# Unrolled expert loop, early output halves, four-bank scatter and ScalarE table loads in a two-layer encoder kernel

## The chip, the cores and the metric

One core of one Trainium2 chip runs the whole program. The metric is device time in microseconds (us) of one execution; lower is better. Engines are named as the profile names them: PE (TensorE matmuls), PEld (TensorE weight loads, which overlap PE), DVE (VectorE), ACT (ScalarE), POOL (GpSimd), SP (SyncE). A "q" behind a name (SPq, PEldq) is the engine's sequencer: its branches, register work and DMA issues.

## The reference

256 tokens of 1024 float32 features pass two layers. Only the last sub-layer and the input matter for the change:

```python
for i in range(DEPTH):                       # DEPTH = 2
    h = rms_norm(x, ln_mix[i])
    x = x + (dilated_attention(h, ...) if i == 0 else rwkv7_bidirectional(h, ...))
    h = rms_norm(x, ln_ffn[i])
    x = x + (swiglu(h, f_w13, f_w2) if i == 0 else moe_swiglu(h, m_router, m_w13, m_w2))

def moe_swiglu(h, router, w13, w2):
    logits = t @ router                      # 8 experts, the two best per token
    combine = softmax over the two, 0 elsewhere
    for e in range(8):
        out = out + combine[:, e:e+1] * swiglu(t, w13[e], w2[e])   # 1024 -> 2 x 3584 -> 1024
```

The kernel takes the rows of a token only to its two experts. Each expert has room for 96 rows (CAP); more go to an overflow loop of at most 5 turns (OVER), and for these inputs it has nothing to do.

## The kernel before

All weights are streamed once from HBM through a ring of R = 6 slots of 2 MB in SBUF. SP issues each unit as two DMAs of 1 MB (`halves`, line 475) after waiting until TensorE is done with the slot's last content (`wait_free`, `wait_free_e`, lines 449 to 462). The order of the work is written out by hand, one block of code for each engine, with semaphores between them.

**Start.** SP issues x in two halves (line 499), then five small tables (lines 500 to 504: the identity matrix and frequencies `const`, the gains `vec`, positions, two tables of QK gains), then the first weight units (line 505 on). VectorE waits for both halves of x and for `vec` (lines 1663 to 1665) ahead of its first instruction; TensorE waits for `const` (line 772), transposes the normalised x (line 695), then starts the QKV projection (line 800) once unit 0 is in its slot.

**Experts.** `expert_plan` gives each expert 21 units: 14 "up" (lines 1252 to 1262, matmuls of lines 1258 and 1261) and 7 "down" (lines 1271 and 1275). Experts 0 to 5 run in a hardware loop of three turns with two experts in each, on TensorE (line 1286), ScalarE (1576) and VectorE (2183). SP's loads run ahead, so the first pair is written out there and the loop of line 643 has two turns. Experts 6 and 7 are written out on every engine. Experts 0 to 6 store their result in DRAM (`yd`) from where GpSimd gathers each token's rows (line 2372); VectorE adds them to x in `add_rows` while TensorE works on expert 7.

**End.** Expert 7's result goes back to x by `scatter` (lines 1235 to 1243): four matmuls, two in each of the PSUM banks 4 and 7, with the third and fourth waiting until VectorE's `add_back` (line 2095) has read the bank. Then each engine reads the number of overflows (`value_load`) and goes five times through the overflow loop, skipping the body each time by a branch. After its loop VectorE raises `experts_done` (line 2199), and SP stores the whole of x in one DMA (line 667) and waits for it.

```python
            with pe.Fori(0, EXPERTS // 2 - 1) as i:          # 1286
                for e in range(2):
                    one_expert(i * 2 + e, e, i)
...
            dve.memset(over_f, 0.0).then_inc(experts_done, 1)   # 2199
...
            sp.wait_ge(experts_done, 1)                         # 666
            sp.dma_start(out.rearrange("(t p) n -> p t n", p=P), x).then_inc(out_done, 16)
            sp.wait_ge(out_done, 16)
```

## Time and profile before

| | us |
|---|---|
| runs, median of 3 (lowest, highest) | 1990.71 (1987.49, 1991.77) |
| the profiled execution | 1985.81 |
| its span in the trace | 1983.9 |
| granted TensorE clock over the span | 0.985 of full speed |
| PE busy | 1886.6 (95%) |
| DVE busy, ACT busy, POOL busy | 703.3, 279.6, 198.3 |
| HBM read | 460.04 MB, 237 GB/s over the span |

The span runs from the first to the last event of the trace; the 1.9 us between it and the execution's time lie around it. The trace gives each instruction's start and length, what released a waiting one, and the chain of releases that ended last. The expert stage runs from about 1025 us to 1969 us, so nearly half of the span.

### The profile page before, as it was taken

What the parts mean: (1) busy time and instruction counts of PE and PEld (TensorE: products, weight loads), DVE (VectorE), ACT (ScalarE), POOL (GpSimd) and SP (SyncE); (2) the same over time, 40 slices, a digit from 0 to 9 for tenths busy, and PEclk for the clock granted to TensorE, in tenths of its full rate; (3) what the DMA queues carried; (4) which work ended last, traced back from release to release, by engine and by line L of the source; (5) the groups of instructions that cost most, each with busy time, mean ns of one, the idle gap of its engine ahead of it and who ended that gap; (6) DMA issues with size and microseconds to landing.
All of it is one profiled execution on the core that took longest, in us unless ns stands there. A gap on an engine that the chain in (4) does not pass through costs nothing.

```text
span 1983.9 us, 42949 instructions
## 1 busy us (share of the span) xinstructions
PE 1886.6 (95%) x18932; PEld 1188.0 (60%) x18932; DVE 703.3 (35%) x2063; ACT 279.6 (14%) x557; POOL 198.3 (10%) x318
## 2 busy tenths in 40 slices
PE   7999998999998999998979999899998999999997
PEld 3445445677754568877665565555555555565554
DVE  3123213100017356675353434233342333424332
ACT  2112112100000324542200000000000000000000
POOL 1111110100001414653010000000000000000000
PEclk9999999999998999999979999999999999999999
DMA  9441441644532100103359999899998999999992
GB/s 360 160 148 65 158 138 43 192 168 146 167 127 85 38 16 16 33 15 94 130 208 405 407 389 398 333 393 379 398 387 331 391 389 394 380 395 397 400 371 89
DMA packets 137658, 472.98 MB, mean 238 GB/s; under 512 B 30104, under 2 KB 59056, under 8 KB 94464
## 3 DMA queue, kind: packets, MB, share of 16 engines
q1 hardware_dynamic: 134592, 460.05, 61.5%
q0 software_dynamic: 2080, 7.37, 1.1%
q8 instruction: 156, 2.56, 0.5%
q10 hardware_dynamic: 800, 2.76, 0.3%
q14 instruction: 30, 0.25, 0.0%
HBM read 460.04 MB, written 10.10 MB: 237 GB/s over the span
## 4 chain that ended last, share of the span: by engine, by line
PE 87%; DVE 6%; ACT 2%; DMA 2%; issue 2%; SPq 0%; POOL 0%; DVEq 0%; POOLq 0%
PE ps L1258 19%; PE ps L678 13%; PE ps L800 13%; PE ps L1261 10%; PE ps L1271 10%; PE ps L738 8%; PE ps L1275 5%; PE ps L751 3%; PE ps L854 1%; PE ps L767 1%; DMA arena<-yd,arena 1%; PE ps L1198 1%; DVE arena L1860 1%; PE ps L686 1%; PE ps L1205 1%
## 5 line engine op out<-in xcount | busy, mean ns | idle before, releaser
L1258 PE MATMUL ps<-arena 128*64 128x256 f32 x3584 | 415.2, 384 | 13.6 <-issue 12.9
L678 PE MATMUL ps<-arena 128*128 128x128 f32 (+11 forms) x2114 | 332.4, 331 | 33.4 <-DVE arena L1847 9.1
L1258 PEld LDWEIGHTS ps<-arena 128*64 128x64 f32 x3584 | 249.0, 138 | 161.3 <-issue 49.6
L678 PEld LDWEIGHTS ps<-arena 128*128 128x128 f32 (+4 forms) x2114 | 247.5, 186 | 110.1 <-issue 55.5
L800 PE MATMUL ps<-arena 128*128 128x512 f32 x576 | 253.1, 595 | 1.9 <-DMA arena<-wqkv 1.9
L2115 DVE TENSOR_TENSOR arena<-arena,ps 64x384 f32<-64x384 f32 x112 | 62.3, 558 | 518.5 <-ACT arena L1560 518.4
L1261 PE MATMUL ps<-arena 128*32 128x128 f32 x7168 | 219.0, 274 | 0.0
L1261 PEld LDWEIGHTS ps<-arena 128*32 128x32 f32 x7168 | 188.9, 110 | 43.1 <-issue 43.1
L1271 PE MATMUL ps<-arena 128*64 128x512 f32 x896 | 207.0, 604 | 4.2 <-DVE arena L2107 4.2
L800 PEld LDWEIGHTS ps<-arena 128*128 128x128 f32 x576 | 108.0, 191 | 128.4 <-issue 125.6
L1560 ACT ACTIVATE arena<-ps 64x384 f32<-64x384 f32 x112 | 54.1, 483 | 799.3 <-PE ps L1261 799.3
L738 PE MATMUL ps<-arena 128*128 128x256 f32 x704 | 153.7, 381 | 0.0
L738 PEld LDWEIGHTS ps<-arena 128*128 128x128 f32 x704 | 134.4, 191 | 20.1 <-issue 1.9
L2106 DVE STREAM_TRANSPOSE arena<-arena 32x128 f32<-32x128 f32 x448 | 136.3, 304 | 9.9
L1271 PEld LDWEIGHTS ps<-arena 128*64 128x64 f32 x896 | 60.1, 138 | 114.4 <-issue 114.4
L1275 PE MATMUL ps<-arena 128*32 128x256 f32 x1792 | 108.3, 382 | 0.0
L1275 PEld LDWEIGHTS ps<-arena 128*32 128x32 f32 x1792 | 52.6, 109 | 74.2 <-issue 45.4
L2107 DVE STREAM_TRANSPOSE arena<-arena 32x64 f32<-32x64 f32 x448 | 87.6, 196 | 0.0
L2372 POOL DMA_INDIRECT arena<-yd,arena x4 | 3.8, 956 | 825.1 <-DMA yd<-arena 824.2
L1656 DVE TENSOR_TENSOR arena<-arena,ps 128x256 f32<-128x256 f32 x22 | 9.3, 421 | 198.4 <-ACT arena L1329 198.4
L1702 DVE TENSOR_REDUCE arena<-arena 128x4 f32<-128x512 f32 x24 | 16.5, 686 | 130.4 <-ACT arena L1354 130.4
L751 PE MATMUL ps<-arena 128*128 128x512 f32 x128 | 55.6, 592 | 0.0
(249 smaller groups left out, 1225.9 us busy)
## 6 DMA issues: line engine op xcount, KB each, us to landing
arena<-mw SPq DMA_DIRECT2D x336, 1024.0 KB, 8.2
arena<-wqkv SPq DMA_DIRECT2D x36, 1024.0 KB, 7.5
arena<-fw SPq DMA_DIRECT2D x32, 1024.0 KB, 6.6
arena<-wrkv SPq DMA_DIRECT2D x12, 1024.0 KB, 7.4
arena<-awo SPq DMA_DIRECT2D x4, 1024.0 KB, 6.3
arena<-bwo SPq DMA_DIRECT2D x4, 1024.0 KB, 9.9
xg<-arena POOLq DMA_DIRECT2D x8, 384.0 KB, 9.0
arena<-xg SPq DMA_DIRECT2D x7, 384.0 KB, 11.5
```

The costliest lines, as they stand in the source:

```text
L678: last = mm(o, a, b, start=(n == 0), stop=(n == len(pairs) - 1))
L738: last = mm(ps[:, c % 4, side * S:(side + 1) * S], w[:, k, side * S + f * P:side * S + (f + 1) * P], src[:, k, :], start=(k == 0), stop=(k ...
L751: last = mm(ps[:, 4 + 2 * t + h, :], hid[:, n % 2, k, t * P:(t + 1) * P], w[:, k, h * 512:(h + 1) * 512], start=(n == 0 and k == 0), stop= ...
L800: last = mm(ps[:, 4 + c % 2, :], hT[:, k, t * P:(t + 1) * P], w[:, k, :], start=(k == 0), stop=(k == KB - 1))
L1258: mm(ps[r, g % 4, 0:256], picked[:, b, k, 0:64], w[:, k, a * 256:(a + 1) * 256], start=(k == 0), stop=(k == KB - 1))
L1261: last = mm(ps[r, g % 4, 256:384], picked[:, b, k, 64:CAP], w[:, k, a * P:(a + 1) * P], start=(k == 0), stop=(k == KB - 1))
L1271: mm(ps[r, 5, :], hidT[:, g % 2, k, 0:64], w[:, k, a * 512:(a + 1) * 512], start=(first and k == 0), stop=(end and k == 3), skip_group_che ...
L1275: last = mm(ps[r, 6, 0:256], hidT[:, g % 2, k, 64:CAP], w[:, k, a * 256:(a + 1) * 256], start=(first and k == 0), stop=(end and k == 3), s ...
L1560: act.activation(sg_e[RH:P, g % 2, :], ps[0:RH, g % 4, 0:3 * P], ACT.Silu).then_inc(sge_sb, 1)
L2106: dve.transpose(o[:, :, :, 32 * i:32 * i + 32], low[:, :, :, j, :])
L2107: last = dve.transpose(o[:, :, i, 64:CAP], high[:, :, j, :])
L2115: dve.tensor_tensor(hid_e[RH:P, pair % 2, g % 2, :], sg_e[RH:P, g % 2, :], ps[RH:P, g % 4, 0:3 * P], ALU.mult).then_inc(hide_sb, 1)
```

## The change

1. ScalarE issues the five small tables, `vec` first, as its first instructions; on SP the first weight unit follows x directly.
2. The loop over experts is gone on TensorE, ScalarE, VectorE and SP: the same three pairs are written out.
3. The scatter writes to banks 4, 7, 0 and 1, and TensorE waits for no addition in between.
4. SP stores x in two halves, each once its own two additions are done, ahead of its overflow loop. A turn of the overflow loop, if one is needed, stores both halves again. `experts_done` is gone.

```diff
@@ SP
             for t in range(T):
                 sp.dma_start(x[:, t, :], x_in[t * P:(t + 1) * P, :]).then_inc(in_x[t], 16)
-            sp.dma_start(const[:, 0:C_TRI], const_in[:, 0:C_TRI]).then_inc(in_const, 16)
-            sp.dma_start(vec, vec_in).then_inc(in_vec, 16)
-            sp.dma_start(pos_i, pos_in).then_inc(in_small, 16)
-            sp.dma_start(qkc, qk_cols).then_inc(in_small, 16)
-            sp.dma_start(qkr, qk_rows.partition_broadcast(P)).then_inc(in_small, 16)
             for u in range(U_QKV):
...
-            with sp.Fori(1, EXPERTS // 2 - 1) as i:
+            for i in range(1, EXPERTS // 2 - 1):
...
+            for t in range(T):
+                sp.wait_ge(back_sb, 2 * t + 2)
+                sp.dma_start(out[t * P:(t + 1) * P, :], x[:, t, :]).then_inc(out_done, 16)
             sp.wait_ge(over_ok, 1)
             many = sp.value_load(over_i[0:1, 0:1], min_val=0, max_val=OVER)
             with sp.Fori(0, OVER) as j:
                 with sp.If(j < many):
...
+                    sp.wait_ge(out_done, j * 32 + 32)
...
+                    for t in range(T):
+                        sp.wait_ge(back_sb, j * 4 + (2 * t + 6))
+                        sp.dma_start(out[t * P:(t + 1) * P, :], x[:, t, :]).then_inc(out_done, 16)
-            sp.wait_ge(experts_done, 1)
-            sp.dma_start(out.rearrange("(t p) n -> p t n", p=P), x).then_inc(out_done, 16)
-            sp.wait_ge(out_done, 16)
+            sp.wait_ge(out_done, 32)
@@ TensorE, scatter
-                    if k >= 2:
-                        pe.wait_ge(back_sb, back * 4 + (k - 5))
-                    run(ps[:, (4, 7)[k % 2], :], [(pickT[0:width, b, t, :], yb[0:width, h * 512:(h + 1) * 512])]).then_inc(back_ps, 1)
+                    run(ps[:, (4, 7, 0, 1)[k], :], [(pickT[0:width, b, t, :], yb[0:width, h * 512:(h + 1) * 512])]).then_inc(back_ps, 1)
@@ TensorE, experts (ScalarE and VectorE likewise)
-            with pe.Fori(0, EXPERTS // 2 - 1) as i:
+            for i in range(EXPERTS // 2 - 1):
                 for e in range(2):
                     one_expert(i * 2 + e, e, i)
@@ ScalarE
+            act.dma_start(vec, vec_in).then_inc(in_vec, 16)
+            act.dma_start(const[:, 0:C_TRI], const_in[:, 0:C_TRI]).then_inc(in_const, 16)
+            act.dma_start(pos_i, pos_in).then_inc(in_small, 16)
+            act.dma_start(qkc, qk_cols).then_inc(in_small, 16)
+            act.dma_start(qkr, qk_rows.partition_broadcast(P)).then_inc(in_small, 16)
@@ VectorE
-                    dve.scalar_tensor_tensor(x[:, t, cols], ps[:, (4, 7)[n % 2], :], weight(t), x[:, t, cols], ALU.mult, ALU.add).then_inc(back_sb, 1)
+                    dve.scalar_tensor_tensor(x[:, t, cols], ps[:, (4, 7, 0, 1)[n], :], weight(t), x[:, t, cols], ALU.mult, ALU.add).then_inc(back_sb, 1)
...
-            dve.memset(over_f, 0.0).then_inc(experts_done, 1)
+                    dve.wait_ge(out_done, j * 32 + 64)
+                    dve.memset(over_f, 0.0)
```

What the compiled programs show. The start of SP's program before, and then of SP's and ScalarE's in the changed kernel (line numbers are each kernel's own; 475 and 474 are the helper that issues weights):

```order
L499 DMA arena<-x 128x1024 x2
L500 DMA arena<-const 128x144
L501 DMA arena<-vec 128x96
L502 DMA arena<-pos 128x2
L503 DMA arena<-qk_cols 128x6
L504 DMA arena<-qk_rows 128x192
L475 DMA arena<-wqkv 128x4x512 x12
L507 DMA arena<-const 128x1730
```

```order
L498 DMA arena<-x 128x1024 x2
L474 DMA arena<-wqkv 128x4x512 x12
L501 DMA arena<-const 128x1730
```

```order
L1309 DMA arena<-vec 128x96
L1310 DMA arena<-const 128x144
L1311 DMA arena<-pos 128x2
L1312 DMA arena<-qk_cols 128x6
L1313 DMA arena<-qk_rows 128x192
L1324 ACT_TABLE_LOAD
L1324 ACTIVATE arena<-arena 128x1024 x2
```

Five issues have gone from between x and the first weights on SP, and stand ahead of ScalarE's first table load.

TensorE at the end of expert 1 (and, in the loop, of 3 and 5), before and then changed. `REGISTER_ALU` and the branch are the loop's; before, the row behind the branch is reached only after the third turn:

```order
L1271 MATMUL ps<-arena 64x512 x8
L1275 MATMUL ps<-arena 32x256 x16
L1286 REGISTER_ALU
L1286 COMPARE_AND_BRANCH
L1258 MATMUL ps<-arena 64x256 x16
```

```order
L1268 MATMUL ps<-arena 64x512 x8
L1272 MATMUL ps<-arena 32x256 x16
L1255 MATMUL ps<-arena 64x256 x16
L1258 MATMUL ps<-arena 32x128 x32
L1255 MATMUL ps<-arena 64x256 x16
```

The next expert's first matmuls now stand directly behind the last of the one before.

TensorE's scatter (the MATMUL rows) before and then changed, followed by SP's end, before and then changed (`[waits ...]` are the semaphores an instruction waits for):

```order
L678 MATMUL ps<-arena 128x512 [waits pickT_sb,result_sb]
L678 MATMUL ps<-arena 128x512
L678 MATMUL ps<-arena 128x512 [waits back_sb] x2
L1294 TENSOR_LOAD arena [waits over_ok]
```

```order
L677 MATMUL ps<-arena 128x512 [waits pickT_sb,result_sb]
L677 MATMUL ps<-arena 128x512 x3
L1291 TENSOR_LOAD arena [waits over_ok]
```

```order
L655 REGISTER_ALU
L655 COMPARE_AND_BRANCH
L667 DMA out<-arena 128x2x1024 [waits experts_done]
```

```order
L649 DMA out<-arena 128x1024 [waits back_sb] x2
L651 TENSOR_LOAD arena [waits over_ok]
```

The store has moved from behind the overflow loop to ahead of it, and is in two pieces.

## Rows read from the trace of the kernel before

**Rows 1.** Page, part 1: busy us of each engine, share of the span, instructions
```profile
PE 1886.6 (95%) x18932; PEld 1188.0 (60%) x18932; DVE 703.3 (35%) x2063; ACT 279.6 (14%) x557; POOL 198.3 (10%) x318
```

**Rows 2.** Chain of waits, expert 1's first matmuls: start us, us, what
```profile
1140.16 3.60 PE ps L1258 x32
```

**Rows 3.** The chain at the first jump back, expert 1 to 2
```profile
1255.15 4.01 issue
1259.16 4.50 PE ps L1258 x24
1263.65 1.82 issue
...
1266.56 1.89 PE ps L1261 x64
```

**Rows 4.** The chain at the second jump back (3 to 4), and leaving the loop
```profile
1492.93 5.50 issue
...
1505.43 1.89 PE ps L1261 x64
...
1731.80 3.60 PE ps L1258 x32
```

**Rows 5.** The loops' branches, on TensorE and VectorE: count, min/median/max ns, starts
```profile
L1286 PEldq COMPARE_BRANCH  x3: 83/5078/6573, 1253.8 to 1730.4; - x3
...
L2183 DVEq COMPARE_BRANCH  x3: 50/56/67, 1255.3 to 1732.0; - x3
```

**Rows 6.** Stretches: us, busy PE, PEld, DVE, ACT, POOL; clock, DMA share, GB/s
```profile
1264.70:1280.70 16.00, 15.22 (x276) 1.00 0.70 263
...
1025.10:1255.10 230.00, 230.00 (x3360) 137.17 (x3360) 93.42 (x372) 14.71 (x30) 4.02 (x4) 1.00 0.98 387
```

**Rows 7.** DMA: issues 1025 to 1060, 1180 to 1255 (us to landing); total 1020 to 1975
```profile
arena<-mw SPq DMA_DIRECT2D x12, 1024.0 KB, 11.0
...
arena<-mw SPq DMA_DIRECT2D x26, 1024.0 KB, 7.9
...
DMA packets 49500, 351.39 MB, mean 368 GB/s; under 512 B 5536, under 2 KB 5536, under 8 KB 7904
```

**Rows 8.** The chain at the start
```profile
1.65 0.42 SPq L500
...
4.01 0.43 SPq L475
...
4.49 9.31 DMA arena<-wqkv
```

**Rows 9.** Timeline at the start: ScalarE's first squares, TensorE's transposes
```profile
4.44 1.06 ACT L1321 ACTIVATE arena<-arena 128x1024 f32<-128x1024 f32 x1 [2.43 <-DMA arena<-x]
...
8.34 3.65 PE L695 MATMUL ps<-arena 128*128 128x128 f32 x16 [8.34 <-DVE arena L1625]
```

**Rows 10.** The stretch in which the small tables arrive (columns of rows 6)
```profile
5.00:8.00 3.00, 0.00 (x0) 0.00 (x0) 0.72 (x2) 2.79 (x5) 0.57 (x1) 1.00 0.91 200
```

**Rows 11.** Timeline of VectorE at the end
```profile
1973.76 1.61 DVE L2095 SCALAR_TENSOR_TENSOR arena<-ps,arena 128x512 f32<-128x512 f32 x2 [0.36 <-PE ps L678]
1979.35 0.07 DVE L2199 MEMSET arena<- 128x11 f32 x1 [3.98 <-issue]
```

**Rows 12.** The end by line: TensorE's and SP's sequencers (ns), the store's landing
```profile
L1294 PEldq TENSOR_LOAD <-arena x1: 487/487/487, 1973.5 to 1973.5; - x1
...
L1297 PEldq COMPARE_BRANCH  x5: 221/221/3520, 1974.5 to 1980.9; - x5
...
L149 PEldq DRAIN  x1: 8/8/8, 1981.5 to 1981.5; - x1
...
L654 SPq TENSOR_LOAD <-arena x1: 480/480/480, 1936.5 to 1936.5; - x1
...
L655 SPq COMPARE_BRANCH  x5: 40/45/54, 1938.1 to 1940.7; - x5
...
DMA to landing us min/median/max: 4.0/4.0/4.0
```

More of the change, by code:

```diff
@@ L364, in build @@
             sem(n) for n in ("up_ps", "sge_sb", "hide_sb", "rows_turned", "hidT_sb", "down_ps", "result_sb", "back_ps", "back_sb"))
-        experts_done = sem("experts_done")
         in_lora, d_ready, mix_ready, mix_ps, mix_sb, ones_ok = (sem(n) for n in ("in_lora", "d_ready", "mix_ready", "mix_ps", "mix_sb", "ones_ok"))
@@ L1575, in _ @@
             act.dma_start(yd[(EXPERTS - 1) * CAP:, :].rearrange("o (a n) -> (o a) n", n=P), zero[0:KB, :]).then_inc(yd_out, 16)
-            with act.Fori(0, EXPERTS // 2 - 1) as i:
+            for i in range(EXPERTS // 2 - 1):
                 for e in range(2):
@@ L2182, in _ @@
             overflow_list()
-            with dve.Fori(0, EXPERTS // 2 - 1) as i:
+            for i in range(EXPERTS // 2 - 1):
                 for e in range(2):
```

## The prediction

> **What bounds the kernel now.** I read the page first: TensorE is busy 1886.6 of 1983.9 us, the next engine 703.3 [rows 1]. So only what makes TensorE pause, and what lies before its first and after its last matmul, can be worth anything here. Then the chain of waits, followed through the expert stage. Within experts it is TensorE's own work without a gap: the first group of an "up" unit takes 3.60 us [rows 2], and the whole first turn of the loop, two experts, takes 230.05 us, from 1025.10 to 1255.15, with TensorE busy throughout [rows 3, 6]. The chain breaks at the loop's jumps back. After expert 1 TensorE has nothing to do for 4.01 us, starts, does 24 matmuls of its first group in 4.50 us, pauses another 1.82 us, and only at 1266.56 reaches the second group [rows 3]. The second jump reads alike: 5.50 us, then the second group at 1505.43 [rows 4]. Where the loop is left, the next group starts at 1731.80 and takes the plain 3.60 us [rows 4].
>
> The rows of the branches say what this is. TensorE's sequencer needs 6573 and 5078 ns for the two branches that go back and 83 ns for the one that falls through; VectorE's need 50 to 67 ns [rows 5]. No semaphore stands behind these waits ("issue"), and the data are there. The Trainium skill, "Runtime: NRT & Kernel Launch", section "Instruction fetch mechanics", has a rule for it: code is fetched ahead in sequence, and a taken branch to a page that isn't held must wait for a fetch. By that rule straight code has none of the pauses, and the skip over the overflow body, also a taken branch, keeps its own. Without it one could as well read the pauses as the price of starting a pair of experts, and the loop's term would be nothing (rival 3). Long for the jumps back and short for the fall-through is what the rule asks for, so the trace agrees.
>
> **The change, part by part.** The durations are those of the profiled execution, 1985.81 us, which is 4.90 us under the median of the runs; the sum is taken from both.
>
> *No loop over experts.* From the end of expert 1 to the second group: 1266.56 - 1255.15 = 11.41 us where 3.60 would do, so 7.81 us lost. At the second jump 1505.43 - 1492.93 = 12.50, so 8.90 us lost. What follows is unharmed: from 1505.43 to 1731.80 are 226.4 us, and the first turn without its first group is 230.05 - 3.60 = 226.4. In the changed program the rows at this place are those of the crossing from expert 0 to 1 or of the fall-through, and neither shows any pause. Gain **16.7 us**. Bounds: 25% more if the pauses of other executions are longer, and 5.5 less if one fetch pause of the longer kind remains: 11 to 21. The loops of the other engines cost TensorE nothing: their branches take at most 67 ns and lie beside 230 us of matmuls.
>
> The cover that could go is the weight stream, since the pauses let it catch up: in the 16 us after the first jump the DMA engines are busy only 0.70 of the time, against 0.98 and 387 GB/s over a turn [rows 6]. I look at the landings. Right after the first pair starts a DMA lands 11.0 us after its issue, 150 us later, with no pause in between, 7.9 us after [rows 7]. A backlog would lengthen these. A slot is issued when the unit six places ahead is done, so it has about five units of 230.05 / 42 = 5.48 us, 27 us. So 27 - 8 = 19 us are in hand, and stay. Cost nothing.
>
> *Tables on ScalarE.* TensorE's transposes end at 8.34 + 3.65 = 11.99 us [rows 9] and its first projection waits to about 13.80 for unit 0, issued from 4.01 us on [rows 8]. In the change unit 0 is issued where L500 stood, at 1.65: 2.36 us earlier, the upper bound. But what moves is the issue, not the transfers: while the tables arrive the DMA engines are already busy 0.91 of the time, at 200 GB/s only [rows 10], because small pieces take engine time too. If none of it overlaps with weights, the gain is the idle part, 0.09 x 3 us = 0.3. If the missing bytes, (387 - 200) / 387 of 3 us, are all filled, it is 1.4. I take **0.9**, between them. The lower end is a loss: identity and `vec` now share the engines with 2 MB of weights, and if the identity took the 9.31 us of [rows 8] from an issue at about 1.2, transposes would run from 10.5 to 14.2, about 0.4 late. On ScalarE the five issues, (4.01 - 1.65) / 5 = 0.47 each, stand ahead of its activation table load and of the squares, which now start at 4.44, when x is in [rows 9]. Should they come 1 us later, the transposes end by 13.0, still about when unit 0 lands; so that costs nothing. Range -0.4 to 2.4. Here the Trainium skill speaks for less than the issue rows promise: "DMA: Bandwidth & Descriptors", section "Issuing engines are not separate DMA queues", says that issuing from several engines saves only the sequencer's time, as all use the same 16 DMA engines. Taken alone it would give the whole 2.4 and a sum 1.5 larger; no run here shows the two queues side by side at the start.
>
> *Four banks.* VectorE's four additions stand in two pairs, the second of 1.61 us, with 0.36 between [rows 11]. Without the wait the last ends some 0.3 earlier, at 1975.07 instead of 1975.37. This counts in the next part.
>
> *The end.* Now: additions end 1975.37, VectorE's five skipped turns to 1979.35, then the store, 4.0 us to landing [rows 11, 12], span 1983.9. Changed: SP issues the second half at about 1975.1, it lands by 1979.1 even at the 4.0 us of the whole, and SP then has its own loop still to go. That took from 1936.5 to 1940.8, 4.3 us, hidden under matmuls [rows 12]; now it starts behind the issue at 1975.6 and ends at 1979.9. VectorE ends at 1979.05. TensorE has the heaviest skip, 3.52 us for its first branch, and drained at 1981.5, having begun to read the count at 1973.5 [rows 12], just behind its waits on the additions. Without these it begins 0.4 to 2.2 us earlier (a matmul's issue, or the start of the scatter), so it ends between 1979.3 and 1981.1. So what was behind the store is late next: SP's loop or TensorE's. Latest of the three about 1980.2, and the closing exchange of signals took 0.4 (the store landed at 1979.45 + 4.0 = 1983.45). New end 1980.6, gain **3.3 us**, from 2.4 to 4.0.
>
> Sum: 16.7 + 0.9 + 3.3 = **20.9 us**. From the profiled execution 1985.81 - 20.9 = 1964.9; from the median 1990.71 - 20.9 = **1969.8 us**. The bounds give 13.0 to 27.4, so 1963.3 to 1977.7.
>
> **The rivals.**
> 1. *Only the loop pays.* Tables and weights get in each other's way at the start, and TensorE's overflow loop, whose skip is a fetch too, ends no earlier than 1983.5. For it: 0.91 busy in [rows 10], 3.52 us in [rows 12]. 16.7 alone: 1974.0.
> 2. *Dearer pauses.* The two pauses differ by 1.1 us, a fetch has to queue behind weight DMAs, and the median lies 4.9 us above the profiled run. If that difference was in the jumps, it goes too: 25.8, 1964.9.
> 3. *The pauses move or stay.* The long straight code could pay for its fetches somewhere else, if the trouble were fetching under full DMA load and not the jump. Against it: 226 us of straight code in each turn have no pause. Then only 4.2 us are gained: 1986.5, at the edge of what counts as no change.
> 4. *Slower: the weights come late.* Without pauses TensorE asks for 387 GB/s over a turn [rows 6], and the stream has no time to catch up. If it held no more than the 368 GB/s that the window of the stage shows as its mean, pauses and ends included, the 351.39 MB [rows 7] would land 955 us after 1020, at 1975, and TensorE would end its last unit one unit later, at 1980.5. It ended about 5 us before the second pair of additions, at 1969 [rows 11]. So 11.5 later, less 4.2 at the ends: 7.3 slower, 1998.0. It decides against the kernel where the last weights land after 1969 + 4.2 - 5.5 = 1967.7, so below 351.39 / 947.7 = 371 GB/s. Against it: the falling landings [rows 7].
>
> **How the numbers follow.** Chances: forecast 0.72, rival 1 0.13, rival 2 0.08, rival 3 0.04, rival 4 0.03. The range 1963.5 to 1977.5 holds the forecast with its bounds and rivals 1 and 2; rivals 3 and 4 stay out. Differences under 0.2%, 4 us, are what a measurement of this kernel can't tell from none. Rivals 1 and 2 are faster by more; rival 3 falls on either side of the bound, half each: faster 0.94, same 0.03, slower 0.03.
>
> **What would show it.** In the changed profile: no "issue" piece between experts 1 and 2 or 3 and 4 and a distance of 115.0 us from each expert's start to the next; landings still near 8 us; the first projection matmul between 12.3 and 13.5; the second output DMA issued within 1 us of the last addition, nothing but sequencer rows after them, TensorE's or SP's loop last. Weight landings that grow to 20 us and TensorE waiting for DMA "mw" would prove rival 4, "issue" pieces inside an expert rival 3.

## The result, and the profile after

The changed kernel takes **1969.49 us** (median of 6 runs, 1964.71 to 1975.43) against 1990.15 (6 runs, 1987.49 to 1994.28): ratio 0.9899, 95% interval 0.9878 to 0.9921, so 20.7 us less by the medians. 1969.8 was forecast. The profiled execution took 1968.82 us with a span of 1967.0; the one of before 1985.81 and 1983.9. That pair is only 17.0 us apart, and its parts don't agree with the terms of the prediction as neatly as the medians do.

First the page's part 1, and of its part 5 (busy us, mean ns | idle just before, and what ended it) three groups of matmuls whose waits matter:

```profile
PE 1883.4 (96%) x18932; PEld 1186.7 (60%) x18932; DVE 703.1 (36%) x2062; ACT 276.8 (14%) x555; POOL 198.0 (10%) x318
...
L1255 PE MATMUL ps<-arena 128*64 128x256 f32 x3584 | 412.5, 382 | 1.1 <-DVE arena L2076 0.7
...
L1258 PE MATMUL ps<-arena 128*32 128x128 f32 x7168 | 221.0, 274 | 2.2 <-issue 2.2
...
L1268 PE MATMUL ps<-arena 128*64 128x512 f32 x896 | 206.3, 603 | 2.4 <-DVE arena L2110 2.4
```

TensorE bounds the kernel as before [rows 1]; it has the same 18932 matmuls and is busy with them for 3.2 us less; the groups behind the jumps, which ran slower (4.50 us for 24 matmuls), are gone. L1255 is line 1258 of the kernel before, the first group of an "up" unit: the page of before has 13.6 us of idle time ahead of it, this one 1.1.

Where the first jump back stood, the chain of waits is now (start us, us, what):

```profile
1251.52 3.58 PE ps L1268 x16
1255.10 1.87 PE ps L1272 x32
1256.97 3.60 PE ps L1255 x32
1260.57 1.88 PE ps L1258 x64
```

Expert 1's last unit ends at 1256.97 and expert 2's first group follows in the plain 3.60 us, where [rows 3] had 4.01 us of "issue", 24 matmuls, and 1.82 more. Those 24 matmuls took 4.50 us where 24 of a plain group's 32 take 2.70: the kernel before's row of that stretch (columns as above [rows 6]) has a granted clock of 0.62, with 3.4 us at half speed in it.

```profile
1259.16:1263.65 4.49, 4.49 (x24) 2.51 (x24) 0.00 (x0) 0.03 (x1) 0.00 (x0) 0.62 0.97 349
```

So of the 7.81 us, 5.83 are pauses and about 1.8 are matmuls at the lower clock. The second place, against [rows 4]:

```profile
1485.08 1.86 PE ps L1272 x32
1486.94 3.60 PE ps L1255 x32
1490.55 1.88 PE ps L1258 x64
```

From expert 1 on, each expert starts 114.99 us after the one ahead of it (I take the starts from its first "up" matmul).

The weights keep up. Stretches of the first two experts and of the 16 us behind them (us; busy PE, PEld, DVE, ACT, POOL; granted clock, DMA share, GB/s), to be read beside [rows 6]:

```profile
1022.94:1252.92 229.98, 228.36 (x3320) 136.43 (x3322) 93.53 (x372) 14.70 (x30) 4.01 (x4) 1.00 0.98 379
1252.92:1268.92 16.00, 16.00 (x246) 9.94 (x244) 2.64 (x6) 2.15 (x4) 0.00 (x0) 1.00 1.00 392
```

The DMA share behind expert 1 is 1.00 (1.00 as well in the stretch 1262.47 to 1278.47, which lies as far behind expert 1 as that of [rows 6]), where it was 0.70: no breathing space is left. Yet the landings, 1180 to 1255 and then over the whole stage (1018 to 1960), answer [rows 7] with

```profile
arena<-mw SPq DMA_DIRECT2D x28, 1024.0 KB, 8.0
...
DMA packets 49639, 351.86 MB, mean 374 GB/s; under 512 B 5549, under 2 KB 5549, under 8 KB 8045
...
arena<-mw SPq DMA_DIRECT2D x324, 1024.0 KB, 8.8
```

8.0 us to landing in the first window, where it was 7.9, and 8.8 over the stage (the pages' part 6 has 8.2 before and 8.8 after, over all 336), against some 27 us that a slot has; the chain holds no wait for them.

The start, first the chain, then TensorE's timeline (in brackets the idle time before and what ended it), against [rows 8, 9]:

```profile
1.65 0.43 SPq L474
...
2.12 11.03 DMA arena<-wqkv
...
13.20 1.98 PE ps L799 x4
```

```profile
8.10 3.53 PE L694 MATMUL ps<-arena 128*128 128x128 f32 x16 [8.10 <-DVE arena L1628]
13.20 1.98 PE L799 MATMUL ps<-arena 128*128 128x512 f32 x4 [1.56 <-DMA arena<-wqkv]
```

Unit 0 is issued 2.36 us earlier and takes 11.03 us instead of 9.31. Of 2.36 us, 1.72 are lost on the way, and the first projection starts 0.64 us earlier. In the stretch 5 to 8 the engines now move 306 GB/s instead of 200, at the same share [rows 10]:

```profile
5.00:8.00 3.00, 0.00 (x0) 0.00 (x0) 0.95 (x3) 2.88 (x5) 0.57 (x1) 1.00 0.91 306
```

The end. VectorE's timeline and SP's, then the rows of the sequencers by line (duration ns min/median/max, first and last start):

```profile
1953.18 1.73 DVE L2131 COPY arena<-ps 32x256 f32<-32x256 f32 x4 [6.61 <-PE ps L1272]
1956.13 3.33 DVE L2098 SCALAR_TENSOR_TENSOR arena<-ps,arena 128x512 f32<-128x512 f32 x4 [1.22 <-PE ps L677]
...
1957.77 2.06 SPq L649 DMA_DIRECT2D out<-arena  x2
```

```profile
L1294 PEldq COMPARE_BRANCH  x5: 221/221/3377, 1956.0 to 1962.3; - x5
...
L649 SPq DMA_DIRECT2D out<-arena x2: 343/343/343, 1957.8 to 1959.5; - x2
...
DMA to landing us min/median/max: 2.6/3.1/3.7
...
L651 SPq TENSOR_LOAD <-arena x1: 545/545/545, 1959.9 to 1959.9; - x1
...
L652 SPq ALU_OP  x5: 33/33/48, 1963.7 to 1966.4; - x5
...
L653 SPq COMPARE_BRANCH  x5: 50/50/63, 1961.3 to 1966.2; - x5
...
L149 PEldq DRAIN  x1: 8/8/8, 1962.8 to 1962.8; - x1
L149 DVEq DRAIN  x1: 17/17/17, 1963.9 to 1963.9; - x1
...
L149 SPq DRAIN  x1: 13/13/13, 1966.8 to 1966.8; - x1
```

The four additions stand as one piece of 3.33 us, without the gap of [rows 11]. SP issues the second half at 1959.5, as the last addition ends (1959.46), and it lands by 1963.2. TensorE is through at 1962.8, VectorE at 1963.9, and SP only at 1966.8. SP skips the overflow body with the branch at 1961.3 and does its next instruction (the counter's addition) at 1963.7: a pause of 2.4 us (from starts given to 0.1 us, as all such pauses below). Before, the same two rows were 1937.5 and 1938.0. SP's loop is what ends the kernel.

Cut at the same four places (expert 0's first "up" matmul, expert 7's, the scatter's first matmul, the end), the spans compare as follows:

| stretch | before | after | gained |
|---|---|---|---|
| start to expert 0 | 1025.10 | 1022.94 | 2.2 |
| expert 0 to expert 7 | 821.62 | 808.89 | 12.7 |
| expert 7 to the scatter | 123.91 | 123.13 | 0.8 |
| scatter to the end | 13.26 | 12.02 | 1.2 |
| span | 1983.9 | 1967.0 | 16.9 |

Three lines ask for an explanation: why experts 0 to 7 give 12.7 and not 16.7, why the end gives 1.2 and not 3.3, and why so much stands in the first line.

### The profile page after: what moved, and what is told of

The parts are those of the page before. It is cut to its first block, busy times and chain, and to the rows that moved or that the text cites. A ratio compares the mean times of both kernels' runs of the same rounds, so it can differ in the third digit from the quotient of the medians.

```text
span 1967.0 us, 42245 instructions
## 1 busy us (share of the span) xinstructions
PE 1883.4 (96%) x18932; PEld 1186.7 (60%) x18932; DVE 703.1 (36%) x2062; ACT 276.8 (14%) x555; POOL 198.0 (10%) x318
## 4 chain that ended last, share of the span: by engine, by line
PE 87%; DVE 6%; ACT 2%; DMA 2%; issue 1%; SPq 0%; POOL 0%; POOLq 0%; DVEq 0%
PE ps L1255 19%; PE ps L677 13%; PE ps L799 13%; PE ps L1258 10%; PE ps L1268 10%; PE ps L737 8%; PE ps L1272 5%; PE ps L750 3%; PE ps L853 2%; PE ps L766 1%; DMA arena<-yd,arena 1%; PE ps L1197 1%; DVE arena L1863 1%; PE ps L685 1%; DMA arena<-wqkv 1%
## 5 line engine op out<-in xcount | busy, mean ns | idle before, releaser
L1255 PE MATMUL ps<-arena 128*64 128x256 f32 x3584 | 412.5, 382 | 1.1 <-DVE arena L2076 0.7
L1255 PEld LDWEIGHTS ps<-arena 128*64 128x64 f32 x3584 | 247.9, 137 | 147.0 <-issue 33.5
```

What stands on the lines that cost most here:

```text
L1255: mm(ps[r, g % 4, 0:256], picked[:, b, k, 0:64], w[:, k, a * 256:(a + 1) * 256], start=(k == 0), stop=(k == KB - 1))
```

## The experiments

Each kernel ran beside the kernel before on the same chip. a_again, a_loop, b_unroll and b_one_jump share one chip; b_pe_unroll, b_tail, a_act_store and a_late_add a second; the other four a third. The kernel before took 1985.48 us on the first (17 runs), 1985.04 on the second (17) and 1986.56 on the third (9); where I turn a ratio into us, it is (1 - ratio) times these.

What the profiled executions show at the places in question (us, from the traces; "lost" is the time from an expert's start to the one two further on, less 229.98; "hidden" is a pause of SP beside the last matmuls):

| kernel | first projection | lost at jump 1, 2 | expert 7 to scatter | scatter to end | SP's first skip |
|---|---|---|---|---|---|
| before | 13.84 | 7.8, 8.9 | 123.9 | 13.3 | 0.5 |
| after | 13.20 | 0, 0 | 123.1 | 12.0 | 2.4 |
| a_again (the same) | 13.43 | 0, 0 | 119.4 | 11.8 | 2.2 |
| a_loop | 12.97 | 7.8, 8.1 | 124.4 | 11.9 | 1.5 |
| b_unroll | 13.77 | 0.3, 0 | 123.3 | 13.3 | 4.6, hidden |
| b_one_jump | 13.81 | 0, 7.4 | 119.8 | 15.1 | 0.5 |
| b_pe_unroll | 13.54 | 0, 0 | 119.0 | 13.3 | 0.5 |
| b_tail | 14.66 | 8.7, 8.1 | 123.7 | 9.7 | 0.5 |
| a_act_store | 13.16 | 0, 0 | 123.9 | 9.6 | 5.2, hidden |
| a_late_add | 12.98 | 0, 0 | 117.3 | 13.4 | 2.2 |
| a_both | 13.20 | 0, 0 | 119.1 | 9.2 | 5.1, hidden |
| b_tables | 13.01 | 9.8, 7.7 | 123.4 | 15.1 | 5.0, hidden |

### a_again: the changed kernel once more

No edit.

> The changed kernel itself once more, to see what belongs to it and what to one execution. In its first profile TensorE slows for about 4 us in expert 0's first two groups (1028.3 to 1032.9, no code fetch and no DMA landing in it), and SP's first skip of the overflow body takes 2.4 us. Theory (straight code keeps no pause): the 4 us slowing is gone or elsewhere, experts 1 to 6 are 115.0 us apart, SP's skip of 2.4 us is there again, ratio to before 0.987 to 0.991. Rival (straight code pays a new pause at its entry): the 4 us are at the same place again. Start: the first projection matmul at 13.2 again; its 32 matmul records take 14.0 if the early clock belongs to the kernel, 15.5 if it is luck.

Measured: 1964.71 us (5 runs), ratio 0.9907 [0.9893, 0.9921]. In its profile all eight experts are 114.99 us apart, expert 0 too, which took 118.98 in the first profile of the same kernel. So 4.0 us of that first profile are not in every execution of the changed kernel; whether the change has a part in them is open (last section). Expert 7 to the scatter took 119.4 us and not 123.1: a second place that varies between executions. The first two projection matmuls are 1.02 us apart here, as in the kernel before, and 0.53 in the first profile: that quicker pace isn't the changed kernel's own.

### a_loop: the changed kernel with its loops over experts back

```
-            for i in range(EXPERTS // 2 - 1):
+            with pe.Fori(0, EXPERTS // 2 - 1) as i:
```

and likewise for ScalarE, VectorE and SP.

> The changed kernel with the loops over experts put back on all engines, all else as changed. Theory (the jumps back cost 7.8 and 8.9 us): 14 to 18 us slower than the changed kernel, the two issue pauses of 4 to 5.5 us after experts 1 and 3 are back, each followed by a pause of 1.5 to 1.8 us after 24 or so matmuls; against before 4 us faster. Rival (the gain came from the start and the end, or from the loads that SP issues without register work): within 4 us of the changed kernel.

Measured: 1982.25 us (11 runs), ratio 0.9987 [0.9979, 0.9996]. Against a_again on the same chip 17.5 us more by the medians, some 16 by the two ratios. The chain at the first jump has both pauses again:

```profile
1252.86 4.31 issue
1257.17 4.41 PE ps L1255 x24
1261.58 1.64 issue
1263.21 1.08 PE ps L1255 x8
```

The two jumps lose 7.8 and 8.1 us. Everything else in the change together is worth 2.6 us [0.8, 4.2].

### b_unroll, b_pe_unroll: the kernel before without loops, and with TensorE's loop alone removed

b_unroll makes the reverse edit of a_loop in the kernel before, on all four engines; b_pe_unroll only this one:

```
-            with pe.Fori(0, EXPERTS // 2 - 1) as i:
+            for i in range(EXPERTS // 2 - 1):
```

> The kernel before with nothing changed but the loops over experts written out on all engines. Theory: 14 to 18 us faster than before, ratio 0.991 to 0.993, no issue pause at the jumps' places, end as before (store behind VectorE's overflow loop). If straight code pays at its entry, 10 to 13 us. Rival: less than 5 us.

> The kernel before with only TensorE's loop written out; ScalarE, VectorE and SP keep theirs. Theory (only TensorE's jumps cost): the same as with all loops written out, 13 to 17 us faster than before, ratio 0.991 to 0.994, experts 115.0 us apart without a gap, although the other engines still jump back. Rival (the register work and jumps of the others delay hidden activations or loads): gaps between experts of some us, and less than 10 us gained.

Measured: b_unroll 1970.56 us, ratio 0.9933 [0.9916, 0.9949], so 13.3 us [10.1, 16.7]; b_pe_unroll 1969.64 us, 0.9923 [0.9906, 0.9940], so 15.3 us [11.9, 18.7]. One row of the page's part 5 tells it, first of the kernel before and then of b_pe_unroll (idle time last):

```profile
L1258 PE MATMUL ps<-arena 128*64 128x256 f32 x3584 | 415.2, 384 | 13.6 <-issue 12.9
```

```profile
L1258 PE MATMUL ps<-arena 128*64 128x256 f32 x3584 | 411.5, 382 | 0.7 <-DVE arena L2073 0.7
```

The idle 12.9 us of "issue" are gone with one engine's loop. The loops of the other engines cost nothing that can be seen (the two intervals overlap), as they had 230 us of matmuls to hide behind.

### b_one_jump: one jump instead of two

```
-            with pe.Fori(0, EXPERTS // 2 - 1) as i:
+            for e in range(2):
+                one_expert(e, e, 0)
+            with pe.Fori(1, EXPERTS // 2 - 1) as i:
```

> The kernel before with TensorE's first pair of experts written out ahead of a loop of two turns, so one jump back instead of two; other engines keep their loops. Theory (each jump back costs about 8 us, and only TensorE's count): one pause, after expert 3, none after expert 1, 7 to 9 us faster than before, ratio 0.9955 to 0.9965. Rival (the price is that of a loop, not of each jump): no faster. Rival (the other engines' loops have part in it): a pause of some us after expert 1 stays.

Measured: 1973.05 us, ratio 0.9942 [0.9929, 0.9954], so 11.5 us [9.1, 14.1]: more than the 7 to 9 expected of one jump. The trace has the mechanism as expected, no pause after expert 1 and one after expert 3:

```profile
1484.21 1.87 PE ps L1275 x32
1486.07 4.94 issue
1491.01 6.10 PE ps L1258 x32
1497.11 1.89 PE ps L1261 x64
```

Here there is no second pause; the 32 matmuls take 6.10 us instead of 3.60, at a granted clock of 0.59 over them, so 4.94 + 2.50 = 7.4 us are lost. The other 4 us of the ratio aren't explained by the jump. In this profile expert 7 has the short form, 119.8 us, where before has 123.9; if it did in most of the runs, that would be it, but single profiles don't show how often it does. (Its long end, 15.1, is the store, which took 5.9 us to land instead of 4.0.) So the size of one jump is taken from the traces, where it is 7.4 to 9.8 us in all nine that there are, and not from this ratio.

### b_tail: only the early halves and the four banks

The core of the edit, in the kernel before:

```
+            for t in range(T):
+                sp.wait_ge(back_sb, 2 * t + 2)
+                sp.dma_start(out[t * P:(t + 1) * P, :], x[:, t, :]).then_inc(out_done, 16)
...
-                    if k >= 2:
-                        pe.wait_ge(back_sb, back * 4 + (k - 5))
-                    run(ps[:, (4, 7)[k % 2], :], ...
+                    run(ps[:, (4, 7, 0, 1)[k], :], ...
```

> The kernel before with the early halves of the store and the four banks alone, loops and tables as before. From the scatter's first matmul to the end of the span: before 13.3 us; in three profiles of kernels with this part 11.8 to 12.0. Theory (SP's own overflow loop, 6.5 us behind the second store, is what ends last): 11.8 again, 1.3 to 1.5 us faster, ratio 0.998 to 1.000. Rival (the predicted 3.3 us): 10.0 us from the scatter to the end.

Measured: 1982.90 us (11 runs), ratio 0.9988 [0.9978, 0.9999], so 2.4 us [0.2, 4.4]. Scatter to end is 9.7 us: 3.6 less than before, 2 less than in the changed kernel, which has the same edit, and 2 less than I expected. SP's rows say why:

```profile
L657 SPq ALU_OP  x5: 33/33/36, 1978.2 to 1980.8; - x5
...
L149 PEldq DRAIN  x1: 8/8/8, 1979.6 to 1979.6; - x1
L149 DVEq DRAIN  x1: 17/17/17, 1980.7 to 1980.7; - x1
...
L149 SPq DRAIN  x1: 13/13/13, 1981.2 to 1981.2; - x1
```

The first skip starts at 1977.7 and the next instruction at 1978.2, 0.5 us, so SP ends 0.5 us behind VectorE. This is the end that the prediction had worked out; the changed kernel misses it by SP's pause.

### a_act_store: the stores on ScalarE

```
-            for t in range(T):
-                sp.wait_ge(back_sb, 2 * t + 2)
-                sp.dma_start(out[t * P:(t + 1) * P, :], x[:, t, :]).then_inc(out_done, 16)
...
+            for t in range(T):
+                act.wait_ge(back_sb, 2 * t + 2)
+                act.dma_start(out[t * P:(t + 1) * P, :], x[:, t, :]).then_inc(out_done, 16)
```

SP is then free for its overflow loop some 40 us earlier.

> The changed kernel with ScalarE issuing the two halves of the store, so that SP goes through its overflow loop while TensorE still works on expert 7. Theory (SP's loop is last): from the scatter to the end 9.3 to 10 us instead of 11.8, bounded by VectorE's loop (7.3 us behind its last addition's start) and the landing of the second half; 2 to 2.5 us faster than the changed kernel. Rival (the landing of the second half decides, or ScalarE's own loop takes SP's place): 11.5 or more.

Measured: 1963.92 us (5 runs), ratio 0.9881 [0.9863, 0.9899]; scatter to end 9.6 us, with the engines through one after another:

```profile
L149 ACTq DRAIN  x1: 8/8/8, 1960.5 to 1960.5; - x1
L149 PEldq DRAIN  x1: 8/8/8, 1960.7 to 1960.7; - x1
L149 DVEq DRAIN  x1: 17/17/17, 1961.5 to 1961.5; - x1
```

SP's first skip took 5.2 us here, from 1919.8 on, under full DMA load, and cost nothing. So SP's pause was what stood between the changed kernel and the forecast end: 2.2 to 2.4 us.

### a_late_add: the routed rows are added later in expert 7

```
-                    if g == 1 and at_second:
+                    if g == 7 and at_second:
```

> The changed kernel with VectorE adding the gathered rows after expert 7's eighth up group instead of its second, when they have long landed. Theory (VectorE blocked on the gather makes TensorE wait 2.3 to 4.5 us in expert 7, and the longer wait lets the granted clock fall to half for a stretch, which is why one expert 7 takes 119.4 and another 123.5 us): expert 7 to the scatter takes 117.0 to 117.5 in every profile, no wait in it, 3 to 7 us faster than the changed kernel and a smaller spread of the runs. Rival (the 5 us of additions now delay hidden activations later): a wait of the same size at expert 7's fourth or fifth down group.

Measured: 1962.32 us (4 runs, 1961.39 to 1963.85), ratio 0.9884 [0.9868, 0.9900]. In a_again's profile TensorE waits for VectorE in expert 7, and in a_act_store's longer. TensorE's timelines there, a_again's first:

```profile
1870.72 3.65 PE L1268 MATMUL ps<-arena 128*64 128x512 f32 x16 [2.06 <-DVE arena L2110]
```

```profile
1871.34 5.99 PE L1265 MATMUL ps<-arena 128*64 128x512 f32 x16 [4.17 <-DVE arena L2110]
```

After a wait of 2.06 us the unit runs at full pace, 3.65 us, at a granted clock of 1.00; after 4.17 us it takes 5.99, at 0.60 (6.02 and 0.60 in the kernel before, after 4.20 us). So 2.1 us more of wait become 4.4 us, the difference between 119.4 and 123.9. The wait's length alone doesn't decide it: a wait of 2.48 us in b_one_jump left the unit at 3.65 us, one of 2.40 in the first profile of the changed kernel was followed by 5.35. The eight profiles that have the additions early and none of the slow places of the last section come in two forms, 119.0 to 119.8 us and 123.3 to 124.4.

Behind the wait stands a gather of routed rows; VectorE's additions, 5.00 us in one piece, begin when it has landed, and the transposes that TensorE needs stand behind them. They began 32.8 us after expert 7's start before and in a_act_store (wait 4.2 us in both), 30.7 in a_again and 30.3 in b_pe_unroll (wait 1.7): of these 2 us the gather's own time to landing, 17.4, 17.2, 16.6 and 16.2 us, is the smaller part, and what leads up to its issue the rest.

With the additions behind the eighth of the fourteen "up" units the wait is gone (117.3 us, 2.1 below the short form). In this profile the scatter took 5.42 us instead of 3.72, at a granted clock of 0.69, and scatter to end is 13.4. That isn't shown to be the edit's doing: a_pad64, the changed kernel as it was, has the same (5.41 us, 0.68, scatter to end 13.3), b_tables too, and a_both, with this edit, doesn't.

### a_both: both of these edits

> The changed kernel with two edits: the four output stores are issued by ScalarE (SyncE's overflow loop then runs early, under matmuls), and the routed rows are added to the result after the last expert's other units (g == 7) instead of after its second. Theory (each edit shortens its own place, the two places don't overlap): from the scatter's first matmul to the end of the span about 9.6 us, as with the ScalarE stores alone (9.56), if TensorE's clock is full there, and from expert 7's first up matmul to the scatter about 117.3 us, as with the late addition alone (117.28), so 2 to 2.3 us less at the end than the changed kernel and 1.5 to 6 us less in expert 7: 1958 to 1962 us, a ratio to the kernel before of 0.986 to 0.988. Rival (the late addition's wait only moves: the scatter then runs right after it at a lower clock, as it took 5.4 us there instead of 3.7): the end is 11 to 11.5 us, no better than either edit alone, ratio 0.988 or more.

Measured: 1964.29 us (5 runs, 1962.29 to 1964.79), ratio 0.9883 [0.9868, 0.9899]. The expected 1958 to 1962 us were missed, and the ratio lies where both the forecast (0.986 to 0.988) and the rival (0.988 or more) end. It is below the changed kernel's 0.9899 and 0.9907, though the intervals overlap, and equal to either edit alone: the sum of the two isn't seen in the time. In the profile the end is the best of all, 9.2 us, so the rival's reason (the wait moves into the scatter) falls. The wait for VectorE in expert 7 is gone too. But 119.1 us, not 117.3, stand between expert 7 and the scatter, and expert 0 takes 118.5. This execution has the same slow place in expert 0 as the first profile of the changed kernel (3.5 us here), and a shorter one early in expert 7. Together they are 5.4 us, as much as the second edit can bring; that they hide the sum in the other four runs too isn't shown. See the last section.

### b_tables: only the small tables and the weights' place

```
-            sp.dma_start(const[:, 0:C_TRI], const_in[:, 0:C_TRI]).then_inc(in_const, 16)
-            sp.dma_start(vec, vec_in).then_inc(in_vec, 16)
...
+            act.dma_start(vec, vec_in).then_inc(in_vec, 16)
+            act.dma_start(const[:, 0:C_TRI], const_in[:, 0:C_TRI]).then_inc(in_const, 16)
...
```

> The kernel before with the small tables loaded by ScalarE and the weights issued right behind x, nothing else. Theory (the transfers share the DMA engines, so most of the 2.36 us of earlier issue is lost): first projection matmul at 13.0 to 13.4 us, against 13.54 to 14.66 in the kernels with the tables on SyncE; about 0.8 us shorter than before in that stretch, not to be told apart in the whole time. Rival (issue order alone counts): first projection matmul at 11.5 us. Rival (identity table comes later and holds up the transposes): 14 us or more.

Measured, one run: 1991.12 us, and the first projection matmul at 13.01. Over all profiles it stands at 12.89 to 13.70 with the tables on ScalarE (nine, mean 13.17) and at 13.54 to 14.66 with them on SP (five, mean 13.92), 0.75 us apart, so both rivals (11.5, and 14 or more) fall. The start of expert 0 is 0.8 us earlier in the mean too (1024.1 against 1025.0), but within either group it varies by 2.9 to 3.5 us. The whole time says nothing: this profile lost 17.5 us at the jumps, 3.5 in expert 0 and 1.9 early in expert 7, and its scatter ran at a granted clock of 0.65 (5.75 us instead of 3.96).

It showed something that it wasn't made for. Its SP has all of before's code but for the five issues at the start, and its first skip of the overflow body, from 1941.4, took 5.0 us instead of 0.5.

### a_pad24, a_pad64: shift SP's code by instructions that do nothing

```
+            for _ in range(24):
+                sp.nop()
```

> The changed kernel with 24 instructions that do nothing on SyncE ahead of its first store. They run while SyncE waits for nothing else of use, before the results are there, so they cost no time themselves; they only shift the code of SyncE's overflow loop by 24 instructions. Theory (the 2.2 to 2.4 us of SyncE's first skip are a fetch of code, and depend on where the jump's target lies to what has been fetched): the pause may stay or go, and the code fetches of the small queue around that moment shift with it; where it goes (0.5 us), SyncE ends some 1.8 us earlier. Rival (the pause is the price of a skip right behind the stores): 2.2 to 2.4 us at the same distance behind the second store, whatever the shift.

> The same with 64 such instructions. Theory (code position): another pause of the first skip than with 0 or with 24 instructions, in at least one of the two runs, 0.5 us where the target is already held; the span's end then is set by TensorE or VectorE and the stretch from the scatter to the end is 10 to 11 us instead of 11.8 to 12.0. Rival (price of a skip behind the stores): 2.2 to 2.4 us in both, 11.8 to 12.0 us.

a_pad64 has 64 of them. Neither profile shows any of these instructions (both count 42245, as many as the changed kernel's), so I take them for two more executions of the changed kernel: 1967.23 and 1967.85 us, with SP pauses of 2.1 us each. Whether the code was moved at all isn't known, so these two runs decide nothing on its position. They do show two more scatter-to-end stretches of this kernel: 11.6 us, and 13.3 with the slow scatter. The theory of the code's position rests on the other kernels: in before, b_one_jump, b_pe_unroll and b_tail, whose SP code is the same up to the last weight units, the skip took 0.5 us, whatever stood around it; in the other eight of the table, where SP has five issues fewer at the start, a loop written out, or both, it took 1.5 to 2.4 us at the end of the kernel and 4.6 to 5.2 us under the weight stream.

## Why the prediction was right, and where not

**The loop, 16.7 us: right in size and cause.** Taking it back costs 17.5 us (a_loop against a_again), taking it out of the kernel before gives 13.3 [10.1, 16.7] and, on TensorE alone, 15.3 [11.9, 18.7]. The forecast's 7.81 and 8.90 us are matched by the traces: 0 and 0 after. The rule of the Trainium skill that it was weighed against ("Runtime: NRT & Kernel Launch", "Instruction fetch mechanics": code is prefetched in sequence, a taken branch to a page that isn't held waits) is borne out by these runs, down to the skip over the overflow body, which stayed: 3377 ns in place of 3520.

The kernel before's trace has the fetches themselves: code transfers of 16 KB on the queue q8. In the changed kernel's straight code, between 1236 and 1274, they come 8.0 to 10.5 us apart and nothing pauses. In the kernel before, at the first jump one starts at 1256.47, inside the pause of 1255.15 to 1259.16, and the next at 1263.22, 0.4 us ahead of the second pause. The first one's line in the DMA view of 1255.2 to 1259.2 (packets, MB, share of 16 engines):

```profile
q8 instruction: 1, 0.02, 1.5%
```

At the second jump of before, the first of a_loop and of b_tables, and the one of b_one_jump one starts in the first pause as well (1495.78, 1254.50, 1260.23, 1488.34). The prediction read the 24 slow matmuls and named no reason; some 1.8 us of each term are the granted clock, which fell to half behind the pause.

Rival 3 (the pauses move or stay) is refuted for the crossings between experts. That rival was right in one corner: pauses of TensorE's supply did show up in straight code, in 5 of 14 profiles, 5.4 to 5.9 us in all; whether the change has a part in them is open.

**The cover, "cost nothing": right.** The DMA engines did lose their rest, 0.70 to 1.00, and the landings stayed near where they were, 8.0 us for 7.9 in one window and 8.8 for 8.2 over all. Rival 4 (weights late, 1998.0) is refuted.

**The tables, 0.9 us: right at the first projection.** 0.64 us in the profiled pair and 0.75 over fourteen profiles, inside a range of -0.4 to 2.4. The choice between the ends, by how much of the engines' time the small pieces leave free, held. That it comes through to the whole time isn't shown. The issue came 2.36 us earlier, but the first unit's transfer took 11.03 us instead of 9.31, beside the tables: that agrees with the Trainium skill ("DMA: Bandwidth & Descriptors", "Issuing engines are not separate DMA queues"), by which transfers issued by several engines interleave on the same 16 DMA engines. The prediction's reading of that section, the whole 2.4 us, took the time saved at issue for time saved at landing. The 2.2 us of the balance's first line are mostly not this term: a_again, the same kernel, reached expert 0 at 1025.30.

**Four banks, 0.3 us: right.** 3.33 us for the four additions instead of 1975.37 - 1971.79 = 3.58 us.

**The end, 3.3 us: the step that failed.** "SP ... starts behind the issue at 1975.6 and ends at 1979.9" took SP's loop over at its old length of 4.3 us. From its load to the end of its last turn it took 1959.9 to 1966.6, 6.7 us: its first skip lasted 2.4 us instead of 0.5, and the way from the load to the first branch 1.4 instead of 0.9. The stretch gave 1.2 to 1.5 us and not 3.3. b_tail, where the skip kept its 0.5 us, gained 3.6 there, so the rest of the working (VectorE and TensorE about 1 us ahead of SP, then 0.4 to close) was sound. Latest was to be about 1980.2, 9.6 us behind the scatter's start; it was 11.6. The prediction counted TensorE's skip as a fetch and took SP's as none, because the row of before was short. By its own argument it could have asked whether a skip is short because it is cheap, or because its target happened to be held.

**Rival 1** (only the loop pays, 1974.0) named the right place for the weak term with the wrong engine: TensorE was through 4.0 us before SP. **Rival 2** (25.8 us, 1964.9) has a_again's time, but its reason (dearer pauses in the median) isn't seen: the jumps cost 7.4 to 9.8 us in every trace, and the kernel before varied by 6.8 us in its 6 runs, of which the two forms of expert 7 could make up some 4.

**The sum.** 20.9 forecast, 20.7 by the medians. The missing 2 us at the end are within what executions vary by: a profile of the changed kernel has none or 5.4 to 5.9 us of supply pauses, and 118.7 to 123.1 us in expert 7. The agreement of the times to 0.3 us is partly luck; that of the loop's term is not. A slip in the chances: with rival 3's 0.04 halved, as the prediction says, they come to faster 0.95 and same 0.02, not 0.94 and 0.03.

## What to carry to other kernels

A backward jump in the engine that bounds the kernel cost 7.4 to 9.8 us each here, over two experts' code and beside a full weight stream, most of it pauses in which a code transfer ran, 1.6 to 2.5 us the lower clock behind them; look for "issue" behind a taken branch, and write such a loop out on that engine alone. Before stores or loops are moved to the end, give each engine's last stretch its price with its fetches at their dearest, and leave what has no hurry (SP's skipped loop) under cover: moving two issues to ScalarE took the stretch from 11.8 or 12.0 to 9.6 us. After a gather, put the consumer where nothing that feeds the busy engine queues behind it: in one pair of profiles here additions that began 2 us later went with 4.4 us more on TensorE.

## What the runs showed of the hardware beyond that

- **A short forward skip turned from cheap to dear with the code ahead of it.** The same branch of SP took 0.5, 1.5 to 2.4, or 4.6 to 5.2 us until the next instruction. In the changed kernel two 8 KB code transfers fall into the pause (1961.7 and 1961.9, pause 1961.3 to 1963.7); b_tables, which differs from before in five issues 1940 us earlier, went from 0.5 to 5.0. In all ten profiles with a long pause, those of a_pad24 and a_pad64 among them, an 8 KB code transfer runs in it; in the four with 0.5 us none does. So the pause is most likely a fetch. What decides whether the target is held wasn't found.
- **TensorE's supply can run dry in straight code.** TensorE's queue of weight loads in expert 0, in the first profile of the changed kernel and then in that of a_again:

```profile
1028.43 0.16 PEld L1258 LDWEIGHTS ps<-arena 128*32 128x32 f32 x4 [0.44 <-issue]
1029.18 0.15 PEld L1258 LDWEIGHTS ps<-arena 128*32 128x32 f32 x4 [0.59 <-issue]
1029.91 0.16 PEld L1258 LDWEIGHTS ps<-arena 128*32 128x32 f32 x3 [0.58 <-issue]
```

```profile
1028.90 1.69 PEld L1258 LDWEIGHTS ps<-arena 128*32 128x32 f32 x64 [0.38 <-issue]
```

  Small groups, 0.74 us from one to the next, at a granted clock of 1.00 and with no wait for data in the rows, for some 5 us; 4.0 us are lost. It happened in 5 of the 14 profiles: the first of the changed kernel and all four of the third chip, with the loop and without (3.5 to 4.0 us), and each time another 1.4 to 1.9 us were lost early in expert 7. In all five it begins at the same matmuls of expert 0, the 80th to 88th, and no 16 KB code transfer starts in it (the nearest are at 1024.04 and 1039.85), so it isn't the pause of a jump. Both places lie beside or just behind GpSimd's indirect DMAs (1027.14 to 1032.07 in expert 0), which the other nine profiles have at the same place. All five have the tables on ScalarE, but four others with them there don't show it. So chip, execution and change aren't separated; it stays open.
- **The pace of the first matmuls differs between executions of one kernel.** The first two projection matmuls were 1.02 us apart in the kernel before and in a_again, 0.53 us in the first profile of the changed kernel, a factor of two at a granted clock that reads 1.00 in all three; the first expert began between 1022.7 and 1026.3 us.
